# Routing in a fused two-block kernel: which engine computes the low parts of 32 weight pieces, and when the routing's steps and its turned indices come

## The chip, the cores and the metric

The kernel runs as one launch on one core of a Trainium2 chip. The metric is the device time in microseconds (us), the median of several executions; smaller is better. The core's engines each run their own instruction stream in order and wait for one another through semaphores: TensorE (PE, matmuls), VectorE (DVE), ScalarE (ACT), GpSimd (POOL) and SyncE (SP), which issues the loads.

## The reference, cut to what matters

Two transformer blocks on 256 tokens with model width 1024. The first ends in a mixture of 16,384 single-vector experts, and that part is the one touched:

```
q = (xt @ wq).reshape(T, 8, 2, 128)
s = einsum('thpd,hpnd->thpn', q, subkeys)             # 8 heads x 2 halves x 128 keys
top_s, top_i = top_k(s, 16)                           # lists of 16, sorted
cand_s = top_s[:,:,0,:,None] + top_s[:,:,1,None,:]    # 16 x 16 candidates a head
best_s, best_j = top_k(cand_s, 16)
idx = take_along_axis(cand_i, best_j); gates = softmax(best_s)
out = sum over the chosen: gelu(x . u_tab[idx]) * gates * v_tab[idx]
```

The kernel gathers nothing. It computes `gelu(x @ u_tab.T)` for all 16,384 experts, multiplies by a dense matrix of gates that is zero where an expert was not chosen, and multiplies by `v_tab`.

## The kernel before, in words

**Pieces.** Every weight streams through the core in pieces of 1 MB (128 partitions x 2048 numbers). To multiply in fp32, each piece is split in two: ScalarE copies it, rounded, into WH (the high part, L1341, helper `hi`), and another engine subtracts, `piece - WH`, into WL (the low part, helper `lo`, L1933 on VectorE, L2775 on GpSimd). Each part comes in two halves of 1024 numbers, one instruction for each half. TensorE then does 48 matmuls for a piece (L594), half of them after each half of the low part. WH and WL have two buffers, so the high part of piece p+2 can be written only when TensorE has used piece p. Three buffers take the loads of this stage. The function `low_on_gpsimd(name, j)` says which pieces have their low part on GpSimd.

**The stage.** `u` has 64 pieces of 256 experts. Pieces 0 to 31 (`up(0)`, `up(1)`) are multiplied while VectorE does the routing; pieces 48 to 63 (`up(3)`) while it builds the gates; then come `v` and the rest. In each program (tensor, scalar, vector) `up` is a generator with four steps to a piece. Where one of its steps takes a piece (`feed.take`), the split of the next piece is issued, so VectorE's low part of piece p+1 stands in its queue ahead of the routing that goes with piece p. ScalarE does a Gelu at a piece's end (L1670) and then the high part of the piece after next.

**Routing.** `routing()` of the vector program has 13 steps for each half of the tokens, 26 in all:
- steps 1 to 4: the sorted lists of the keys, four at a time: MAX8 (L2445), FIND_INDEX8 (L2448), MATCH_REPLACE8 (L2452) over 128 numbers
- steps 5 and 6: the candidates (a sum of 128x1024, L2464) and their sorted lists over 256 numbers; step 5 starts with a cast of the indices (L1921)
- step 7: the best scores less the first (L1906); ScalarE takes the exponent (L1333, its own routing step 7, which stands in its queue behind the Gelu of the seventh piece, and for the second half behind that of the twentieth); VectorE waits for it and divides
- steps 8 to 10 and 11 to 13: look up the two indices with wide one-hot tables of 128x2048: compare (L1906), multiply (L2492), sum (L2495)

One step goes with each piece. After piece 27 TensorE turns the indices and gates so that tokens lie along the free axis (`ids`, L1171), VectorE copies them (`ids`) and builds the first rows of the gates (`early_rows`, 20 steps, L2361 and L2367) beside pieces 28 to 31, at 1.25 steps for each step of `up`.

**Names below.** "Piece p" is the u piece of that number, from 0. "T6" is the time at which the Gelu of piece 6 starts, which is the end of that piece's matmuls.

Of the kernel before, what the change touches and what calls it, by code (L numbers as in the profile page):

```python
# [64 lines left out]
DOTS = ((0, 0, 0, 2, 0, 0, 0, 2, 0, 2, 0, 2), (0, 2, 0, 0) * 2 + (0, 2) * 2, (0, 2, 0, 0) * 2 + (0, 2) + (0,) * 6)  # L65
UNITS = ((2,) * 12, (1,) * 8 + (2,) * 4, (1, 0) * 5 + (1, 2, 2, 2, 2, 0))
HEADS = (3,) * 11 + (0,) * 5


def of_chunks(name, js):  # L70
# [117 lines left out]
class Marks:  # L188
# [5 lines left out]
    def on(self, name):  # L194
        if self.dry:
            return self.at.get(name, (self.zero, 1))
        return self.at[name]
# [62 lines left out]
class Mem:  # L260
# [42 lines left out]
    def tile(self, name):  # L303

        return self.ps[self.marks.bank.get(name, 0)][:, :]
# [156 lines left out]

def low_on_gpsimd(name, j):

    return name == "in_g" or name == "u" and j < 28 and j % 4 != 3


def split_views(m, n, name, j):
# [76 lines left out]
def chain(*gens):  # L545
    for g in gens:
        yield from g


def some(steps, n=1):  # L550
    for _ in range(n):
        next(steps, None)


def finish(steps):
    for _ in steps:
        pass


def beside(main, side, ratio):  # L560
    due = 0.0
    for _ in main:
        due += ratio
        while due >= 1:
            due -= 1
            next(side, None)


def tensor_program(q, m):
# [17 lines left out]
    def bank(name, of=ring):  # L587
        b = of["ids"][of["at"] % len(of["ids"])]
        of["at"] = (of["at"] + 1) % len(of["ids"])
        return give(b, name)  # L590

    def mm(o, pairs, start=True, stop=True, skip=False):
        for i, (l, r) in enumerate(pairs):
            ins = q.matmul(o, l, r, start=start and i == 0, stop=stop and i == len(pairs) - 1, skip_group_check=skip)  # L594
        return ins
# [60 lines left out]
    def proj(name, k0, *need, by=None):  # L656
        finish(proj_steps(name, k0, *need, by=by))
# [138 lines left out]
    def barrier(n):  # L796
        p.mark(("all", n, "pe"))
# [188 lines left out]
    def front():  # L986
# [54 lines left out]
        for i, _ in enumerate(states()):  # L1041
            some(fill, UNITS[2][i])
            some(dots, DOTS[2][i])
            some(at, HEADS[i])
            if i == 9:
# [46 lines left out]
    def up(b_):  # L1092

        for r in range(16):
            n, h, l, halves = take()
            tile = ("up", b_, r)
            b = bank(tile)
            for i, (x, z) in enumerate(halves):
                p.wait_ge(*on(("lo", n, i)))
                for e in range(2):  # L1100
                    fs = slice(e * P, (e + 1) * P)
                    ins = mm3(b[:, e * T:(e + 1) * T], [(h[:, k, fs], l[:, k, fs], RH[:, k, :], RL[:, k, :])
                                                        for k in range(x, z)], start=i == 0 and e == 0,
                              stop=i == 1 and e == 1, skip=True)
                    if e == 0:
                        yield
                ins.then_inc(*p.up(tile))
                p.mark(("used", n, i))
                yield

    def gate():

        for t in range(0, T, 4):
            b = bank(("gate", t), gate_ring).rearrange("p (i t) -> p i t", t=4)
            p.wait_ge(*on(("rows j", t // 8 * 8)))
            p.wait_ge(*on(("rows i", t)))
            for j in range(4):
                if t % 16 + j < 2:
                    l, r = m.early_j[:, t // 16, j, :], m.early_i[:, t // 16, j, :]
                else:  # L1120
                    l, r = m.rows_j[t // 8 % 2][:, t % 8 + j, :], m.rows_i[t // 4 % 3][:, j, :]
                ins = mm(b[:, :, j], [(l, r)])
            ins.then_inc(*p.up(("gate", t)))
            yield
# [24 lines left out]
    def peer():  # L1149
        proj("wq", 0, by="xs2")  # L1150
        feed.take()
        p.wait_ge(*m.loaded(CHUNKS.index(("sub", 0))))
        p.wait_ge(*on(("out", ("wq", 14))))
        sub = m.chunk(CHUNKS.index(("sub", 0)))
        for tt in range(2):
            for g in range(0, 16, 4):
                tile = ("keys", tt, g)
                b = bank(tile)
                for k in range(4):
                    ins = mm(b[:, k * P:(k + 1) * P], [(m.Qp[:, g + k, tt * P:(tt + 1) * P], sub[:, (g + k) * P:(g + k + 1) * P])])  # L1160
                ins.then_inc(*p.up(tile))
        p.mark("sub used")
        ring["ids"], ring["at"] = [0, 1, 2, 3], 0
        finish(up(0))
        steps = up(1)
        some(steps, 48)
        for tt in range(2):
            b = bank(("ids", tt))
            p.wait_ge(*on("routed"))
            for i in range(3):  # L1170
                ins = q.transpose(b[:, i * P:(i + 1) * P], m.res[tt][i], ident)  # L1171
            ins.then_inc(*p.up(("ids", tt)))
        finish(steps)
        g = gate()
        beside(up(3), g, 1)
        finish(g)
        for i in range(4):
            p.wait_ge(*on(("out", holder[4 + i])))
        finish(down(1))
        finish(up(2))  # L1180
        finish(down(0))
        finish(down(2))
        finish(down(3))
        for i in range(4):
            holder[4 + i] = ("down", i)
        banks = [bank(("turn back", k)) for k in range(0, 8, 2)]
        for tt in range(2):
            p.wait_ge(*on(("out", ("down", 2 * tt))))
            p.wait_ge(*on(("out", ("down", 2 * tt + 1))))
            for k in range(8):  # L1190
                o = k % 2 * T + tt * P
                ins = q.transpose(banks[k // 2][:, o:o + P], m.ot[:, tt, k * P:(k + 1) * P], ident)
                if tt == 1 and k % 2 == 1:
                    ins.then_inc(*p.up(("turn back", k - 1)))
        ring["ids"], ring["at"] = list(range(7)), 0
        barrier(2)
# [126 lines left out]
def scalar_program(q, m):  # L1323
# [110 lines left out]
    def front():  # L1434
# [107 lines left out]
        for i in range(16):  # L1542
            some(fill, UNITS[2][i])
            some(at, HEADS[i])
            some(dots, DOTS[2][i])
# [353 lines left out]
def vector_program(q, m):  # L1899
# [19 lines left out]
    def CP(o, x, name=None):  # L1919
        v.wait_ge(*v.last())  # L1920
        q.tensor_copy(o, x).then_inc(*v.up(name))  # L1921
# [16 lines left out]
    def proj(name, each=None):  # L1938
        finish(walk(name, feed, each))
# [29 lines left out]
    def rest_of_pair(tag, src, k):  # L1969

        v.wait_ge(*on((tag, "hi", k)))
        q.tensor_tensor(RL[:, k:k + 2, :], src[:, k:k + 2, :], RH[:, k:k + 2, :].bitcast(F32),
                        ALU.subtract).then_inc(*v.up((tag, "half", k // 4)))
        v.mark((tag, "pair", k // 2))
# [44 lines left out]
    def front():  # L2019
# [106 lines left out]
        for i, _ in enumerate(states()):  # L2126
            some(fill, UNITS[2][i])
            some(at, HEADS[i])
            some(dots, DOTS[2][i])
# [220 lines left out]
    def up(b_):  # L2350

        for _ in range(16):
            yield
            feed.take()
            yield
            yield
            yield
# [140 lines left out]
    def peer():  # L2498
        proj("wq")
        feed.take()  # L2500
        v.wait_ge(*on(("out", ("keys", 1, 12))))
        r = routing()
        beside(up(0), r, 0.25)
        steps = up(1)
        beside((next(steps) for _ in range(48)), r, 0.25)
        finish(r)
        for tt in range(2):
            t = ("ids", tt)
            ts = slice(tt * P, (tt + 1) * P)
            v.wait_ge(*on(t))  # L2510
            CP(m.ids[:, :, ts], tile(t)[:, 0:384].rearrange("p (a t) -> p a t", a=3), ("out", t))
        v.wait_ge(*v.last())
        early = early_rows()
        beside(steps, early, 1.25)
        finish(early)
        g = gate()
        beside(up(3), g, 1)
        finish(g)
        finish(down(1))
        finish(up(2))  # L2520
        g = far_gated()
        beside(down(0), g, 0.5)
        finish(g)
        finish(down(2))
        finish(down(3))
        for tt in range(2):
            v.wait_ge(*on(("down tokens", tt)))
            CP(m.ot[:, tt, 0:512], m.ps[4 + tt * 2][:, :], ("out", ("down", tt * 2)))
        for k in range(0, 10, 2):
            t = ("turn back", k)  # L2530
            if k < 8:
                v.wait_ge(*on(t))
                for g in range(2):
                    q.scalar_tensor_tensor(m.X[:, k + g, :], tile(t)[:, g * T:(g + 1) * T], mod[:, 40 + k + g:41 + k + g],
                                           m.X[:, k + g, :], ALU.mult, ALU.add).then_inc(*v.up(("x peer", k + g)))
                v.mark(("out", t))
            if k > 0:
                rest_of_pair("xs3", m.X, k - 2)
        v.mark("xs3")
        barrier(2)  # L2540
# [519 lines left out]
```

## Time and profile before

| | us |
|---|---|
| median of 3 executions | 1754.6 (1752.82 to 1759.29) |
| profiled execution, its own time | 1753.6 |
| its span | 1751.8 |
| TensorE busy | 1658.0 (95%) |
| VectorE busy | 1141.3 (65%) |
| ScalarE busy | 818.3 (47%) |
| GpSimd busy | 152.1 (9%), 58 low-part halves |

TensorE is busy nearly all the time, and the chain that ended last lies on it for 79% of the span. Its mean granted clock is 0.965 of full speed. What is left is the time in which it waits, or runs at the lower clock after a wait. GpSimd does nothing but low parts: 16 halves in an earlier stage and 42 in this one. Times in the rows count from the start of the span; the routing runs from 460 to 622 us, pieces 0 to 31 from 460 to 663.

### The profile page before, as it was taken

To read this page: it belongs to the slowest core of one execution; us is meant where nothing else is said; L and a number is where in the kernel's file an instruction comes from. 1 tells how busy PE (TensorE), PEld (TensorE's weight loads), DVE (VectorE), ACT (ScalarE), POOL (GpSimd) and SP (SyncE) were. 2 spreads that over 40 slices of the span, in tenths; PEclk is the share of its full clock that TensorE was granted. 3 is DMA by queue.
4 is the path that set the end of the run, shared out by engine and by line. 5 is a ranking of instruction groups with operands and counts; after the bars stand their busy time and mean duration, and the time that the engine had idled before them with its cause. 6 is when DMAs were issued, how large, how long until landed. Compare 5 with 4: busy or idle time off the path is not lost.

```text
span 1751.8 us, 27228 instructions
## 1 busy us (share of the span) xinstructions
PE 1658.0 (95%) x11462; PEld 1508.3 (86%) x11462; DVE 1141.3 (65%) x1961; ACT 818.3 (47%) x1187; POOL 152.1 (9%) x62
## 2 busy tenths in 40 slices
PE   6989999898989999999999999999999998999998
PEld 4879887798989999998889988888898787999996
DVE  5775865565497969997544477555575464556675
ACT  4635433334444444444444444444434655555663
POOL 0001231000356630000000000000000000000000
PEclk8999987899989999999999999999999998999999
DMA  9524323244435455455565586555655354445331
GB/s 388 209 103 150 140 97 121 97 145 144 169 123 190 169 171 175 166 175 181 192 224 185 181 288 234 195 193 196 256 190 175 116 180 145 165 137 183 121 123 70
DMA packets 48462, 300.57 MB, mean 172 GB/s; under 512 B 5586, under 2 KB 6098, under 8 KB 15827
## 3 DMA queue, kind: packets, MB, share of 16 engines
q1 hardware_dynamic: 43442, 290.28, 47.3%
q10 hardware_dynamic: 4896, 8.54, 1.3%
q8 instruction: 90, 1.47, 0.3%
q14 instruction: 34, 0.27, 0.0%
HBM read 288.18 MB, written 9.44 MB: 170 GB/s over the span
## 4 chain that ended last, share of the span: by engine, by line
PE 79%; DVE 13%; ACT 4%; POOL 2%; DMA 1%; issue 1%; SPq 0%; DVEq 0%; ACTq 0%
PE ps L594 78%; DVE WL L1933 3%; POOL WL L2775 2%; DVE ar L1906 2%; ACT ar L1333 1%; DVE ar L2448 1%; DVE ar L2445 1%; DVE ar L1917 1%; ACT WH L1341 1%; DVE ar L2452 1%; DVE ar L2232 1%; DMA vec<-in_vec 0%; DVE ar L1925 0%; DMA ar<-in_in_rkv 0%; DVE ar L2464 0%
## 5 line engine op out<-in xcount | busy, mean ns | idle before, releaser
L1933 DVE TENSOR_TENSOR WL<-ar,WH 128x1024 fp32r<-128x1024 f32 (+1 forms) x420 | 495.5, 1208 | 365.8 <-ACT WH L1341 365.2
L594 PE MATMUL ps<-RH,WH 128*128 128x256 f32 x2136 | 632.8, 296 | 34.7 <-DVE WL L1933 15.3
L594 PE MATMUL ps<-RL,WH 128*128 128x256 f32 x2136 | 614.5, 288 | 0.0
L594 PE MATMUL ps<-RH,WL 128*128 128x256 f32 x2136 | 614.1, 287 | 0.0
L1341 ACT ACTIVATE WH<-ar 128x1024 fp32r<-128x1024 f32 (+1 forms) x478 | 481.8, 1041 | 274.7 <-PE ps L594 258.6
L594 PEld LDWEIGHTS ps<-RH,WH 128*128 128x128 f32 x2136 | 420.0, 197 | 42.5 <-issue 12.7
L594 PEld LDWEIGHTS ps<-RL,WH 128*128 128x128 f32 x2136 | 420.1, 197 | 0.9 <-issue 0.2
L594 PEld LDWEIGHTS ps<-RH,WL 128*128 128x128 f32 x2136 | 419.6, 196 | 0.0
L594 PE MATMUL ps<-WH,RH 128*128 128x512 f32 (+1 forms) x832 | 325.5, 391 | 11.3 <-DVE ar L1917 5.9
L594 PE MATMUL ps<-WL,RH 128*128 128x512 f32 (+1 forms) x832 | 322.0, 387 | 0.0
L594 PE MATMUL ps<-WH,RL 128*128 128x512 f32 (+1 forms) x832 | 321.7, 387 | 0.0
L594 PE MATMUL ps<-ar 128*128 128x128 f32 (+8 forms) x2124 | 246.4, 299 | 21.5 <-DVE ar L1921 10.9
L594 PEld LDWEIGHTS ps<-ar 128*128 128x128 f32 (+6 forms) x2124 | 204.8, 177 | 48.7 <-issue 27.2
L594 PEld LDWEIGHTS ps<-WH,RH 128*128 128x128 f32 x832 | 157.5, 189 | 45.0 <-DVE ar L1917 6.0
L2775 POOL TENSOR_TENSOR WL<-ar,WH 128x1024 fp32r<-128x1024 f32 x58 | 151.9, 2642 | 476.0 <-ACT WH L1341 476.0
L594 PEld LDWEIGHTS ps<-WL,RH 128*128 128x128 f32 x832 | 157.7, 190 | 31.6 <-issue 1.0
L594 PEld LDWEIGHTS ps<-WH,RL 128*128 128x128 f32 x832 | 157.6, 189 | 31.7
L1670 ACT ACTIVATE ar<-ps 128x512 f32<-128x512 f32 x64 | 38.2, 597 | 178.2 <-PE ps L594 178.2
L1333 ACT ACTIVATE ar<-ps 128x256 f32<-128x256 f32 (+3 forms) x156 | 71.9, 461 | 92.3 <-PE ps L594 78.3
L1906 DVE TENSOR_TENSOR ar<-ps,ar 128x512 f32<-128x512 f32 (+3 forms) x59 | 38.4, 651 | 65.1 <-PE ps L594 58.4
L2361 DVE TENSOR_SCALAR ar<-con,ar 128x128 f32<-128x128 f32 x256 | 71.3, 340 | 0.0
L1333 ACT ACTIVATE ar<-ar,small 128x128 f32<-128x128 f32 (+1 forms) x48 | 21.9, 455 | 62.2 <-DVE small L1994 61.4
(155 smaller groups left out, 956.1 us busy)
## 6 DMA issues: line engine op xcount, KB each, us to landing
ar<-in_u SPq DMA_DIRECT2D x64, 1024.0 KB, 4.9
ar<-in_v SPq DMA_DIRECT2D x64, 1024.0 KB, 4.9
ar<-in_adr SPq DMA_DIRECT2D x16, 1024.0 KB, 5.3
ar<-in_ada SPq DMA_DIRECT2D x8, 1024.0 KB, 12.7
ar<-in_in_g SPq DMA_DIRECT2D x8, 1024.0 KB, 4.9
ar<-in_wq SPq DMA_DIRECT2D x8, 1024.0 KB, 4.9
far_gates<-ar ACTq DMA_DIRECT2D x32, 256.0 KB, 2.3
ar<-far_gates SPq DMA_DIRECT2D x16, 512.0 KB, 3.9
```

What stands on the lines that cost most here:

```text
L594: ins = q.matmul(o, l, r, start=start and i == 0, stop=stop and i == len(pairs) - 1, skip_group_check=skip)
L1333: q.activation(o, x, f, **k).then_inc(*a.up(name))
L1341: q.activation(h[:, x:z, :], src[:, x:z, :], ACT.Copy).then_inc(*a.up(("hi", n, i)))
L1670: q.activation(m.H[:, i0:i0 + 2, :], tile(t).rearrange("p (n t) -> p n t", n=2), ACT.Gelu).then_inc(*a.up(("out", t)))
L1906: q.tensor_tensor(o, x, y, op).then_inc(*v.up(name))
L1917: q.scalar_tensor_tensor(o, x, s, y, op0, op1).then_inc(*v.up(name))
L1933: q.tensor_tensor(l[:, x:z, :], src[:, x:z, :], h[:, x:z, :].bitcast(F32), ALU.subtract).then_inc(*v.up(("lo", n, i)))
L2232: q.scalar_tensor_tensor(x, x, 1.0, m.cwide, ALU.mult, ALU.mult, accum_out=mod[:, i:i + 1]).then_inc(*v.up(("adr", j)))
L2361: return q.tensor_scalar(o, cst("iota"), m.ids[:, 0, t:t + 1], m.ids[:, 2, t:t + 1], ALU.is_equal, ALU.mult)
L2445: q.max(vals[:, s8], src).then_inc(*v.up())
L2448: q.max_index(idx[:, s8], vals[:, s8], src).then_inc(*v.up())
L2775: q.tensor_tensor(l[:, x:z, :], src[:, x:z, :], h[:, x:z, :].bitcast(F32), ALU.subtract).then_inc(*g.up(("lo", n, i)))
```

## The change

Four edits, all in how work is placed:
- GpSimd's pieces: before all but every fourth of pieces 0 to 27 (21 pieces); now pieces 0 to 7 and 12 to 20 (17 pieces). VectorE has pieces 8 to 11 and 21 to 31 (before 3, 7, 11, 15, 19, 23, 27 to 31).
- The routing steps on VectorE go by a table: one with each of pieces 0 to 9, three with piece 10, one with each of 11 to 18, none with piece 19, one with each of 20 to 24.
- TensorE turns the indices after piece 25, and VectorE waits for them there.
- The early rows go beside pieces 26 to 31 at 0.875 a step.

ScalarE's program has the same order as before. The file's lines move down by 3 to 5.

```diff
+ROUTED = (1,) * 10 + (3,) + (1,) * 8 + (0,) + (1,) * 5
 def low_on_gpsimd(name, j):
-    return name == "in_g" or name == "u" and j < 28 and j % 4 != 3
+    return name == "in_g" or name == "u" and (j < 8 or 12 <= j < 21)
@@ tensor program
         steps = up(1)
-        some(steps, 48)
+        some(steps, 40)
@@ vector program
         r = routing()
-        beside(up(0), r, 0.25)
-        steps = up(1)
-        beside((next(steps) for _ in range(48)), r, 0.25)
+        steps = chain(up(0), up(1))
+        for n in ROUTED:
+            some(steps, 4)
+            some(r, n)
         finish(r)
+        some(steps, 4)
...
         early = early_rows()
-        beside(steps, early, 1.25)
+        beside(steps, early, 0.875)
```

VectorE's queue where the first half of the tokens passes from the sorted lists to the look-ups, before. L1933 is a low part (piece 7's in the fourth row), L2473 is the first instruction behind ScalarE's exponent:

```order
L2452 MATCH_REPLACE ar<-ar 128x256 x4
L2445 MAX ar<-ar 128x8 x4
L2448 MAX_INDEX ar<-ar 128x8 x4
L1933 TENSOR_TENSOR WL<-ar,WH 128x1024 x2
L1906 TENSOR_TENSOR ar<-ar 128x128
L2473 TENSOR_REDUCE small<-ar 128x8
L1925 RECIPROCAL small<-small 128x8
L1906 TENSOR_TENSOR ar<-ar,small 128x128
L2483 TENSOR_SCALAR ar<-ar 128x128
L1921 CAST ar<-ar 128x128
L1906 TENSOR_TENSOR ar<-ar,con 128x2048
L2492 TENSOR_TENSOR ar<-ar 128x2048
```

The same place now (L1936 is the low part, of pieces 8 and 9 here; the other lines are 3 higher too):

```order
L2455 MATCH_REPLACE ar<-ar 128x256 x4
L2448 MAX ar<-ar 128x8 x4
L2451 MAX_INDEX ar<-ar 128x8 x4
L1909 TENSOR_TENSOR ar<-ar 128x128
L2476 TENSOR_REDUCE small<-ar 128x8
L1928 RECIPROCAL small<-small 128x8
L1909 TENSOR_TENSOR ar<-ar,small 128x128
L1936 TENSOR_TENSOR WL<-ar,WH 128x1024 x2
L2486 TENSOR_SCALAR ar<-ar 128x128
L1924 CAST ar<-ar 128x128
L1909 TENSOR_TENSOR ar<-ar,con 128x2048
L1936 TENSOR_TENSOR WL<-ar,WH 128x1024 x2
```

No low part stands among the lists now; the first one (piece 8's) stands behind the four instructions around the exponent, and each look-up step has one ahead of it.

VectorE's queue at the same place for the second half of the tokens, before (the low part is that of piece 23):

```order
L1906 TENSOR_TENSOR ar<-ar 128x128
L2473 TENSOR_REDUCE small<-ar 128x8
L1925 RECIPROCAL small<-small 128x8
L1906 TENSOR_TENSOR ar<-ar,small 128x128
L2483 TENSOR_SCALAR ar<-ar 128x128
L1921 CAST ar<-ar 128x128
L1906 TENSOR_TENSOR ar<-ar,con 128x2048
L2492 TENSOR_TENSOR ar<-ar 128x2048
L1933 TENSOR_TENSOR WL<-ar,WH 128x1024 x2
L2495 TENSOR_REDUCE ar<-ar 128x128
```

And now (the low parts are those of pieces 21, 22 and 23):

```order
L1909 TENSOR_TENSOR ar<-ar 128x128
L2476 TENSOR_REDUCE small<-ar 128x8
L1928 RECIPROCAL small<-small 128x8
L1909 TENSOR_TENSOR ar<-ar,small 128x128
L2486 TENSOR_SCALAR ar<-ar 128x128
L1924 CAST ar<-ar 128x128
L1909 TENSOR_TENSOR ar<-ar,con 128x2048
L1936 TENSOR_TENSOR WL<-ar,WH 128x1024 x2
L2495 TENSOR_TENSOR ar<-ar 128x2048
L1936 TENSOR_TENSOR WL<-ar,WH 128x1024 x2
L2498 TENSOR_REDUCE ar<-ar 128x128
L1936 TENSOR_TENSOR WL<-ar,WH 128x1024 x2
```

Piece 21's low part has come from GpSimd into VectorE's queue, behind the exponent and the first wide comparison. On TensorE six transposes stand 96 matmuls (two pieces) sooner, and nothing else moved there.

## Rows read from the trace of the kernel before

**Rows 1.** Busy time of each engine by stretch, then granted clock, DMA share, GB/s.
```profile
500.00:520.00 20.00, 12.23 (x85) 12.22 (x85) 19.35 (x41) 7.86 (x9) 7.12 (x3) 0.74 0.31 106
580.00:600.00 20.00, 17.82 (x135) 17.53 (x134) 19.31 (x43) 10.35 (x12) 13.61 (x5) 0.91 0.46 154
620.00:640.00 20.00, 18.66 (x157) 18.67 (x157) 6.69 (x7) 8.57 (x11) 8.29 (x4) 1.00 0.60 206
680.00:700.00 20.00, 20.00 (x175) 20.00 (x174) 20.00 (x49) 8.77 (x15) 0.00 (x0) 1.00 0.53 174
```
**Rows 2.** TensorE's waits, 459 to 664 us: total, times, longest.
```profile
PE ps L594 <- DVE WL L1933: 7.8, 1, 7.8
PE ps L594 <- POOL WL L2775: 4.6, 4, 2.2
```
**Rows 3.** Timeline of ScalarE: start, length, instruction, [idle before, releaser].
```profile
465.53 0.60 ACT L1670 ACTIVATE ar<-ps 128x512 f32<-128x512 f32 x1 [3.86 <-PE ps L594]
...
500.08 0.60 ACT L1670 ACTIVATE ar<-ps 128x512 f32<-128x512 f32 x1 [3.27 <-PE ps L594]
500.76 1.28 ACT L1333 ACT_TABLE_LOAD   x1
509.16 0.31 ACT L1333 ACTIVATE ar<-ar 128x128 f32<-128x128 f32 x1 [7.12 <-DVE ar L1906]
509.38 1.99 ACT L1341 ACTIVATE WH<-ar 128x1024 fp32r<-128x1024 f32 x2
...
515.98 0.60 ACT L1670 ACTIVATE ar<-ps 128x512 f32<-128x512 f32 x1 [3.31 <-PE ps L594]
...
586.17 0.60 ACT L1670 ACTIVATE ar<-ps 128x512 f32<-128x512 f32 x1 [3.46 <-PE ps L594]
...
601.57 0.60 ACT L1670 ACTIVATE ar<-ps 128x512 f32<-128x512 f32 x1 [5.32 <-PE ps L594]
...
638.90 0.60 ACT L1670 ACTIVATE ar<-ps 128x512 f32<-128x512 f32 x1 [3.27 <-PE ps L594]
...
645.30 0.60 ACT L1670 ACTIVATE ar<-ps 128x512 f32<-128x512 f32 x1 [3.91 <-PE ps L594]
...
662.58 0.60 ACT L1670 ACTIVATE ar<-ps 128x512 f32<-128x512 f32 x1 [3.27 <-PE ps L594]
```
**Rows 4.** Timeline of VectorE, 472 to 520 us.
```profile
472.86 2.36 DVE L1933 TENSOR_TENSOR WL<-ar,WH 128x1024 fp32r<-128x1024 f32 x2 [2.87 <-ACT WH L1341]
475.26 0.87 DVE L2445 MAX8 ar<-ar 128x8 f32<-128x128 f32 x4
...
480.07 0.88 DVE L2445 MAX8 ar<-ar 128x8 f32<-128x128 f32 x4
...
484.89 2.09 DVE L1921 CAST ar<-ar 128x256 f32<-128x256 uint32 x1
487.02 3.31 DVE L2464 TENSOR_TENSOR ar<-ar 128x1024 f32<-128x1024 f32 x1
...
497.85 1.23 DVE L2464 TENSOR_TENSOR ar<-ar 128x1024 f32<-128x1024 f32 x1
...
506.46 2.34 DVE L1933 TENSOR_TENSOR WL<-ar,WH 128x1024 fp32r<-128x1024 f32 x2
...
512.99 4.38 DVE L1906 TENSOR_TENSOR ar<-ar,con 128x2048 f32<-128x2048 f32 x1
517.41 2.29 DVE L2492 TENSOR_TENSOR ar<-ar 128x2048 f32<-128x2048 f32 x1
519.73 2.29 DVE L2495 TENSOR_REDUCE ar<-ar 128x128 f32<-128x2048 f32 x1
```
**Rows 5.** Timeline of GpSimd: low parts of pieces 4 and 5, and of 9 and 10.
```profile
478.67 4.79 POOL L2775 TENSOR_TENSOR WL<-ar,WH 128x1024 fp32r<-128x1024 f32 x2 [6.75 <-ACT WH L1341]
484.43 4.82 POOL L2775 TENSOR_TENSOR WL<-ar,WH 128x1024 fp32r<-128x1024 f32 x2 [0.97 <-ACT WH L1341]
...
517.61 11.45 POOL L2775 TENSOR_TENSOR WL<-ar,WH 128x1024 fp32r<-128x1024 f32 x4 [2.38 <-ACT WH L1341]
```

## The prediction

> **What bounds the kernel now.** I read the stretches first: TensorE should show where it is not full. In three of them it is not [rows 1]: 12.23 of 20 us with the clock at 0.74, then 17.82 at 0.91, then 18.66 at 1.00. From 680 us on it is full again, and VectorE too. Its waits come next: all of them between 459 and 664 us are for low parts, 7.8 us once for VectorE and 4.6 us in four waits for GpSimd [rows 2]. So in this stage neither loads nor high parts come last, only low parts.
>
> Then the Gelus, which mark the ends of pieces [rows 3]. T0 is 465.53 and T6 is 500.08, so a piece without a wait takes 34.55/6 = 5.76 us. Pieces 1 to 31 would take 31 x 5.76 = 178.6 us; they took 662.58 - 465.53 = 197.05. So 18.5 us are lost here, and that is all that this change can give in the stage. They split so: piece 7 took 15.90, lost 10.1; pieces 20 and 21 took 15.40, lost 3.9; piece 28, behind which the turning of the indices stands, took 6.40, lost 0.6; the rest, 3.9, is spread over pieces 9, 12, 19, 22, 24 and 25.
>
> The timelines of VectorE and GpSimd say why [rows 4, 5]. Piece 7's low part is VectorE's. TensorE wanted it at 500.08, and it started at 506.46, since in VectorE's queue it stands behind the candidates and their lists, which ran late. The wait costs 7.8; the other 2.3 are the lower clock after it (0.74 over 20 us is 5.2 us lost at full-speed count, of which about half fell into the wait itself). And ops of VectorE with two inputs in the core's memory take turns with GpSimd's: the sum of 128x1024 took 1.23 alone and 3.31 beside a low part of GpSimd, the comparison of 128x2048 took 4.38 where the multiplication took 2.29, and the latter held GpSimd up in its turn (four halves in 11.45 instead of 2 x 4.79 = 9.58). The sorted lists don't take turns: four MAX8 took 0.87 with GpSimd idle and 0.88 beside the low part that ran from 478.67 to 483.46. Nor does the sum of the look-up, 2.29 with GpSimd busy.
>
> The Trainium skill (SBUF — State Buffer, section "Who interferes with whom") says that an instruction of VectorE with two inputs there contends with GpSimd's reads. By that rule FIND_INDEX8 and MATCH_REPLACE8, if their loaded values count as a second input, would contend too, and this change, which puts GpSimd beside all the lists, would slow them. The list step from 480.07 to 484.89 had GpSimd beside it most of the time and took 4.82; the one from 475.26 to 480.07 had it for 1.4 us and took 4.81. The trace decides: no contention.
>
> **The change part by part.** I carry the schedule on with durations of these rows. VectorE: low part 2.34 to 2.36 for both halves (1.2 each), list step over 128 numbers 4.82, over 256 numbers 497.85 - 490.33 = 7.5, look-up 2.29, with two small ones of about 0.25 ahead of each comparison. GpSimd: 2.4 a half, 4.8 a piece, starting 1.6 us after T (484.43 against T3 = 482.8). VectorE can give the first half of a low part at T+2.8.
>
> *Pieces 3 and 7 to GpSimd.* 4.8 us a piece against 5.76: GpSimd keeps up, its first half at T+4.0, 1.8 before it is wanted. VectorE loses the low part of piece 3 and the wait ahead of it (2.36 + 2.87 [rows 4]), so step 5 starts at 484.89 - 5.2 = 479.7. Its cast waits for GpSimd until 481.06 (as in the row), its sum until 483.46 and ends about 484.5; lists to 492.0. Step 6: the sum waits 0.6 for the half that began at 490.2, ends 493.7; lists to 501.2. GpSimd, held up 1.1 by this sum, ends piece 7's first half at 498.4 and its second at 500.8: before 500.08 and 503.0, when TensorE wants them. So T7 = 500.08 + 5.76 = 505.84, and the 10.1 us go.
>
> *The exponent.* ScalarE has its table loaded at 502.04 at the earliest [rows 3], VectorE's scores are there at 501.5. Exponent 502.04 to 502.35, high part of piece 8 to 504.3, low part on VectorE 503.4 to 505.8, first half at 504.6. Wanted at 505.84: no wait. ScalarE's wait of 7.12 goes too.
>
> *Pieces 8 to 11 on VectorE between the look-ups.* Each piece now needs on VectorE a low part and a look-up, 2.35 + 2.29 = 4.6, with a comparison 5.2, under 5.76, and nothing of GpSimd's beside it. Following it: piece 9's low part ends 511.0 (T8 = 511.6), 10's 515.7, 11's 521.4 (T10 = 523.1). The three steps with piece 10 end at 528.9. The comparison and the multiplication there hold GpSimd from 524.8 to 526.5, so piece 12's first half comes at 528.9, just when TensorE wants it (T11 = 528.9). I take 0.1 us lost. The losses at pieces 9 and 12 go.
>
> *Lists of the second half.* No low part on VectorE until piece 21, so it runs ahead: from 528.9, 4 x 4.82, then two candidate steps with turns of 2 to 4 us, in all to about 569. Then it waits for the exponent, which stands on ScalarE behind the Gelu of piece 19: T19 = 528.95 + 8 x 5.76 = 575.0, Gelu 0.6, table 1.28, exponent from 577.0 to 577.3. **Here is the new wait.** Piece 21's low part is queued behind it: the rest of step 20 to 578.2, the small ones and the comparison to 581.1, low part's first half at 582.3. TensorE wants it at T20 = 580.8 and starts about 582.4: 1.6 us lost. A wait of 2.2 at most was followed by a slower clock before (0.91 over 580 to 600, or 3.6 us at half speed, 1.8 lost), one inside 620 to 640 was not, with 1.34 us idle at clock 1.00 [rows 1, 2]. 1.6 lies between: 0 to 1.8, I take 0.9. What went away here: the 3.9 of pieces 20 and 21, and the late ones of 22, 24 and 25, all due to GpSimd taking turns with look-ups; pieces 22 to 26 now go by the 4.6 to 5.2 of VectorE and catch up, the last look-up ending at about 606, T25 at about 611.
>
> *Turning two pieces sooner.* The indices are ready 5 us ahead of T25, so TensorE doesn't wait. The 0.6 of piece 28 comes with piece 26. VectorE copies, then has six low parts (14.1) and 20 early steps (13.4, from 0.26 us a row and 1.2 a comparison) in six pieces, 34.6: fits. It can start the gates' rows a little before T31 instead of just after; in the gates' stage TensorE and VectorE are both full [rows 1], so I count 0, at most 0.6.
>
> *Loads* wait for the low part three pieces back. That of a GpSimd piece ends at T+6.4 where VectorE's ended at T+3.9; a load takes about 5 us (page, DMA issues), and the high part wants it 17 us after that T: hidden, with 5 us in hand.
>
> **Sum.** Lost before 18.5; lost after 0.6 + 0.1 + 1.6 + 0.9 = 3.2. Gain 15.3. The profiled execution had 1753.6, so 1738.3; the median of the runs is 1.0 above that execution and their lowest 0.8 below it. I say 1738.5. All later stages are ordered by the same engines and move as a block. The case's own range, with the clock from 0 to 1.8, the gates' 0.6, and 1.5 for a median of other executions: 1735.5 to 1741.
>
> **Rivals.**
> 1. *The exponent of the first half is late.* Four ops ahead of it take turns (cast, two sums, scores); I counted 3.8 us of turns, the most is 4 x 2.4 = 9.6. Then the scores come at 507, piece 8's high part waits behind the exponent, and its low part's first half comes at 508.7 against 505.84: 2.9 lost, and about 1.9 by the clock. Gain 10.5: 1743. For it: in the row both ops at 484.89 and 487.02 waited a full turn. Against: the second sum at 497.85 met none, and GpSimd is idle when the scores come.
> 2. *The look-ups with low parts between them bind.* VectorE, not TensorE, sets the pace of pieces 8 to 11 and 21 to 31, since each low part must wait for its high part and each look-up for the one before. The price is what a piece on VectorE takes over 5.76; it decides at 16/15 = 1.1 us a piece over, i.e. 6.8. At 7.3 (as piece 25 had) 15 x 1.55 = 23 lost against 15.3 won: slower, 1761. For it: 19.35 of 20 us busy on VectorE [rows 1]. Against: the row's own durations give 5.2, and much of that busy time is turns.
> 3. *It only moves the wait.* The second exponent costs the whole of what pieces 20 and 21 lost and more, since the rest of step 20 and the comparison stand ahead of the low part: a wait of 4 with 2.5 of clock, and the same at piece 12. Gain 15.3 + 2.5 - 2 x 5 = 8: 1746. Against: nothing in the rows makes the comparison longer than 2.3 without GpSimd.
>
> The Trainium skill (GPSIMD Engine Reference, section "Key points") says that VectorE is structurally about twice as fast at elementwise work. The trace agrees, 1.2 against 2.4 us a half; it matters only where GpSimd has no slack, and by the rows it has 1.0 a piece.
>
> **Chances.** Forecast 0.76; rival 1 0.12; rival 3 0.08, half of it under the bound of 0.5% (8.8 us, about what a measurement of this kernel can tell from no change); rival 2 0.02; 0.02 for anything else, as a later stage giving the time back. Faster 0.93, same 0.05, slower 0.02. Range, to take in most of rival 1: 1735 to 1743.5.
>
> **What would show it.** Piece 7 at 5.8 us; ScalarE's exponent within 2.5 us of the seventh Gelu; MAX8 and the rest of the lists at the same length beside GpSimd; wide comparisons and multiplications at 2.29 and not 4.38; a single wait of TensorE for VectorE, 1 to 2 us, at piece 21; T31 near 647.4. It is wrong if piece 8 or 12 shows a wait over 1 us, if pieces 22 to 25 take over 6, or if the gates' stage takes longer than 9.31 us a piece.

## The result, and the profile after

| | before | after |
|---|---|---|
| first comparison, median of 7 each (us) | 1757.33 (1752.37 to 1759.29) | 1744.41 (1738.02 to 1748.25) |
| ratio, 95% interval | | 0.9929 (0.9914 to 0.9945) |
| second comparison, ratio | | 0.9934 (0.9909 to 0.9959) |
| profiled execution, its own time | 1753.6 | 1747.57 |

The kernel got faster by 0.7%. The forecast was 1738.5 with a range to 1743.5, so the measured 1744.41 lies 0.9 above the range and 5.9 above the forecast. Inside the stage nearly every number of the forecast came out.

TensorE's waits from 470 to 660 us in the changed kernel (columns as in [rows 2]):

```profile
PE ps L597 <- ACT WH L1344: 1.6, 1, 1.6
```

Five waits of 12.4 us in all [rows 2] have become one of 1.6. ScalarE around the first exponent, piece 12, and the second exponent (to set beside [rows 3]):

```profile
509.57 0.60 ACT L1673 ACTIVATE ar<-ps 128x512 f32<-128x512 f32 x1 [3.27 <-PE ps L597]
510.25 1.28 ACT L1336 ACT_TABLE_LOAD   x1
511.55 0.31 ACT L1336 ACTIVATE ar<-ar 128x128 f32<-128x128 f32 x1
511.76 1.99 ACT L1344 ACTIVATE WH<-ar 128x1024 fp32r<-128x1024 f32 x2
513.77 1.28 ACT L1673 ACT_TABLE_LOAD   x1
515.34 0.60 ACT L1673 ACTIVATE ar<-ps 128x512 f32<-128x512 f32 x1 [0.28 <-PE ps L597]
...
538.37 0.60 ACT L1673 ACTIVATE ar<-ps 128x512 f32<-128x512 f32 x1 [3.26 <-PE ps L597]
...
544.41 0.60 ACT L1673 ACTIVATE ar<-ps 128x512 f32<-128x512 f32 x1 [3.55 <-PE ps L597]
...
584.74 0.60 ACT L1673 ACTIVATE ar<-ps 128x512 f32<-128x512 f32 x1 [3.27 <-PE ps L597]
585.41 1.28 ACT L1336 ACT_TABLE_LOAD   x1
586.70 0.31 ACT L1336 ACTIVATE ar<-ar 128x128 f32<-128x128 f32 x1
586.92 1.99 ACT L1344 ACTIVATE WH<-ar 128x1024 fp32r<-128x1024 f32 x2
588.93 1.28 ACT L1673 ACT_TABLE_LOAD   x1
590.49 0.60 ACT L1673 ACTIVATE ar<-ps 128x512 f32<-128x512 f32 x1 [0.28 <-PE ps L597]
590.99 2.00 ACT L1344 ACTIVATE WH<-ar 128x1024 fp32r<-128x1024 f32 x2
598.05 0.60 ACT L1673 ACTIVATE ar<-ps 128x512 f32<-128x512 f32 x1 [5.06 <-PE ps L597]
```

T6 is 509.57 here and T7 515.34: piece 7 takes 5.77 where it took 15.90. The exponent follows the Gelu and the table at once, with no wait for VectorE (7.12 before). Piece 12 takes 6.04 and piece 21 takes 598.05 - 590.49 = 7.56. VectorE at the same places ([rows 4]):

```profile
489.14 1.57 DVE L1924 CAST ar<-ar 128x256 f32<-128x256 uint32 x1
490.74 3.31 DVE L2467 TENSOR_TENSOR ar<-ar 128x1024 f32<-128x1024 f32 x1
494.09 1.41 DVE L2448 MAX8 ar<-ar 128x8 f32<-128x256 f32 x4
...
501.57 1.61 DVE L2467 TENSOR_TENSOR ar<-ar 128x1024 f32<-128x1024 f32 x1
...
510.69 0.29 DVE L1909 TENSOR_TENSOR ar<-ar 128x128 f32<-128x128 f32 x1
511.89 0.28 DVE L2476 TENSOR_REDUCE small<-ar 128x8 f32<-128x128 f32 x1 [0.91 <-ACT ar L1336]
...
517.97 2.35 DVE L1936 TENSOR_TENSOR WL<-ar,WH 128x1024 fp32r<-128x1024 f32 x2
520.36 2.29 DVE L2495 TENSOR_TENSOR ar<-ar 128x2048 f32<-128x2048 f32 x1
...
587.05 0.29 DVE L2476 TENSOR_REDUCE small<-ar 128x8 f32<-128x128 f32 x1 [6.67 <-ACT ar L1336]
...
588.46 2.29 DVE L1909 TENSOR_TENSOR ar<-ar,con 128x2048 f32<-128x2048 f32 x1
590.67 2.35 DVE L1936 TENSOR_TENSOR WL<-ar,WH 128x1024 fp32r<-128x1024 f32 x2
```

The look-ups take 2.29 between low parts. The cast and the first sum wait for GpSimd, the second sum for 0.4. The scores are ready 1.4 us after T6. For the second half of the tokens VectorE waits 6.67 for the exponent, and the comparison and then the low part of piece 21 stand behind it. TensorE wanted that low part at 590.5 and its first half ended at 591.9. The list of waits names ScalarE's high part, but that of piece 21 had been done since 588.9; what came last is the low part, as the run with the two exchanged shows below. GpSimd beside the first lists, and the two pieces after the look-ups ([rows 5]):

```profile
488.16 4.81 POOL L2780 TENSOR_TENSOR WL<-ar,WH 128x1024 fp32r<-128x1024 f32 x2 [0.98 <-ACT WH L1344]
493.92 4.77 POOL L2780 TENSOR_TENSOR WL<-ar,WH 128x1024 fp32r<-128x1024 f32 x2 [0.95 <-ACT WH L1344]
...
534.24 11.09 POOL L2780 TENSOR_TENSOR WL<-ar,WH 128x1024 fp32r<-128x1024 f32 x4 [24.02 <-ACT WH L1344]
```

It has 0.95 to 0.99 us in hand at a piece beside the lists. It is held up at three places: half a piece took 3.41 instead of 2.41 beside the second sum of each half of the tokens, and beside the look-ups that go with piece 10 four halves took 11.09 instead of 9.6. Behind piece 21's wait the clock stayed up (columns of [rows 1]):

```profile
590.00:592.00 2.00, 0.45 (x4) 0.25 (x4) 2.00 (x3) 1.72 (x4) 0.00 (x0) 1.00 0.00 0
592.00:594.00 2.00, 1.97 (x16) 2.00 (x17) 1.97 (x2) 0.98 (x2) 0.00 (x0) 1.00 0.00 0
594.00:596.00 2.00, 2.00 (x19) 2.00 (x18) 2.00 (x2) 0.00 (x0) 0.00 (x0) 1.00 0.95 291
```

The Gelus are counted on through the gates' stage: its 16 pieces end at T32 to T47, and behind T47 the multiplication by `v` begins (the down stage, below). Four parts make up a profiled execution: T0; the stage, T31 - T0; the gates' stage, T47 - T31, which is 148.6 before and 148.0 after in every profile (the gates start 0.59 sooner); and what lies behind T47.

| | T0 | T31 - T0 | behind T47 | T0 and behind T47 together |
|---|---|---|---|---|
| before, first profile | 465.53 | 197.05 | 940.62 | 1406.15 |
| after, first profile | 475.01 | 181.27 | 941.39 | 1416.40 |

The stage and the gates gave 15.78 + 0.59 = 16.4 us; the rest of the kernel, with the same instructions, took 10.2 us more. Ten of the sixteen runs below go to that question.

### The profile page after: what moved, and what is told of

It reads as the page before. It is cut to its first block, busy times and chain, and to the rows that moved or that the text cites. A ratio compares the mean times of both kernels' runs of the same rounds, so it can differ in the third digit from the quotient of the medians.

```text
span 1745.7 us, 27230 instructions
## 1 busy us (share of the span) xinstructions
PE 1670.6 (96%) x11462; PEld 1514.7 (87%) x11462; DVE 1138.4 (65%) x1969; ACT 819.4 (47%) x1187; POOL 123.8 (7%) x54
## 4 chain that ended last, share of the span: by engine, by line
PE 86%; DVE 8%; ACT 4%; DMA 2%; issue 1%; SPq 0%; DVEq 0%; ACTq 0%
PE ps L597 85%; DVE WL L1936 2%; DVE ar L1909 2%; ACT ar L1336 1%; DVE ar L1920 1%; DMA ar<-in_cwide 1%; ACT WH L1344 1%; DMA vec<-in_vec 0%; PE ps L778 0%; DMA ar<-in_in_rkv 0%; DVE ar L2235 0%; DVE ar L1928 0%; DVE ar L2065 0%; DVE RL L1952 0%; ACT L1336 0%
## 5 line engine op out<-in xcount | busy, mean ns | idle before, releaser
L1936 DVE TENSOR_TENSOR WL<-ar,WH 128x1024 fp32r<-128x1024 f32 (+1 forms) x428 | 503.4, 1205 | 347.7 <-ACT WH L1344 346.9
L597 PE MATMUL ps<-ar 128*128 128x128 f32 (+8 forms) x2124 | 255.9, 312 | 19.2 <-DVE ar L1924 10.1
L597 PEld LDWEIGHTS ps<-ar 128*128 128x128 f32 (+6 forms) x2124 | 210.1, 183 | 50.9 <-issue 31.4
L2780 POOL TENSOR_TENSOR WL<-ar,WH 128x1024 fp32r<-128x1024 f32 x50 | 123.6, 2494 | 461.4 <-ACT WH L1344 461.4
```

Of the source, the lines that this page charges most:

```text
L1936: q.tensor_tensor(l[:, x:z, :], src[:, x:z, :], h[:, x:z, :].bitcast(F32), ALU.subtract).then_inc(*v.up(("lo", n, i)))
L2780: q.tensor_tensor(l[:, x:z, :], src[:, x:z, :], h[:, x:z, :].bitcast(F32), ALU.subtract).then_inc(*g.up(("lo", n, i)))
```

## The experiments

The stage's length repeats to 0.04 us over seven profiles of the changed kernel and to 0.8 us over five of before (196.3 or 197.1, by what piece 7 takes), so the stage's theories are told apart by one profile; the medians of whole executions are far coarser.

| kernel | T31 - T0 | pieces over 5.8 us | ratio to before, interval |
|---|---|---|---|
| before, 5 profiles | 196.26 to 197.06 | 7, 9, 12, 19 to 22, 24, 25, 28 | 0.9996 (0.998 to 1.0011) |
| after, 7 profiles | 181.25 to 181.29 | 12, 21, 26 | 0.9934 (0.9909 to 0.9959) |
| e3, pieces only | 179.47 | 12, 28 | 0.9898 (0.9873 to 0.9923) |
| e4, steps only | 194.83 | 7, 9, 12, 19 to 22, 24, 26 | 0.9994 (0.998 to 1.0007) |
| e5, piece 7 only | 194.31 | 7, 8, 9, 12, 19 to 22, 24, 25, 28 | 0.9996 (0.998 to 1.0011) |
| e6, comparison behind low part | 179.46 | 12, 26 | 0.9907 (0.9884 to 0.993) |
| e7, also piece 12 | 179.20 | 26 | 0.9911 (0.9893 to 0.993) |
| e8, GpSimd beside look-ups | 211.87 | 14 pieces | 1.0081 (1.0055 to 1.0106) |

The lengths of pieces go by the Gelus. Where ScalarE is late itself, a part of a wait is counted one piece too early: before the change piece 20 shows 7.59, though TensorE's wait of 2.18 us stands ahead of piece 21.

**The pieces alone (e3).** The kernel before with

```diff
-    return name == "in_g" or name == "u" and j < 28 and j % 4 != 3
+    return name == "in_g" or name == "u" and (j < 8 or 12 <= j < 21)
```

> Only the pieces' engines change (GpSimd has 0 to 7 and 12 to 20); one routing step with each piece and the turning behind piece 27 stay as before. Theory (all of the gain is in which pieces GpSimd has, and the changed kernel's one wait, at piece 21, comes from a table that puts the wide comparison ahead of piece 21's low part): here the low part stands ahead of the comparison, so no wait at piece 21. T31 - T0 = 178.6 + 0.3 (piece 12) + 0.6 (turning) = 179.5; gates' start 0.6 later than in the changed kernel; in all 1 us faster than the changed kernel. Rival (the step table and the earlier turning carry a part of the gain): T31 - T0 of 184 or more.

Measured 179.47, and no wait at piece 21: the theory. One of the four edits carries all of the stage's gain, and more: the changed kernel's step table costs it 1.8 us. What the earlier turning gives is the 0.59 at the gates' start, which e3 lacks.

**The steps and the turning alone (e4).** The changed kernel with the pieces' rule of before and `ROUTED = (1,) * 20 + (2,) + (1,) * 4`.

> The pieces' engines stay as before; only the steps and the turning move: one routing step with each of pieces 0 to 19, two with 20, one with 21 to 24, turning behind piece 25, early rows at 0.875. (The changed kernel's own table would wait in a ring here: it puts step 20, which waits for ScalarE behind the Gelu of piece 19, ahead of piece 19's low part on VectorE.) Theory (the pieces carry the gain): piece 7 takes 15.9 as before, T31 - T0 = 197 within 3, the gates' start 0.6 sooner; the time is that of before within 3 us. Rival (turning sooner carries a part): T31 - T0 under 193.

Piece 7 took 15.22, the stage 194.83, the gates came 0.6 sooner, and the ratio is that of no change: the theory. Against the 196.3 of before with the same piece 7, 1.4 us go, mainly at piece 25, whose low part no longer comes late.

**Piece 7 alone (e5).** The kernel before with `j < 28 and (j % 4 != 3 or j == 7)`.

> The kernel before with only piece 7 given to GpSimd beside its others. Theory (the wait of 7.8 at piece 7 goes only in part, since VectorE, with piece 3's low part still among the lists and turns with GpSimd, has the scores at 506.5 on the scale of before, and piece 8's high part waits on ScalarE behind the exponent): piece 7 takes 5.8, piece 8 about 12 (wait 4.8, clock 2), so T31 - T0 is 3 to 4 us shorter than 197.05. Rival (the low part of piece 7 was all of it): piece 8 takes 5.8 and T31 - T0 is 10 us shorter.

TensorE's waits, and ScalarE around the exponent:

```profile
PE ps L594 <- POOL WL L2775: 9.6, 4, 5.3
```

```profile
501.36 0.60 ACT L1670 ACTIVATE ar<-ps 128x512 f32<-128x512 f32 x1 [3.27 <-PE ps L594]
502.04 1.28 ACT L1333 ACT_TABLE_LOAD   x1
508.55 0.31 ACT L1333 ACTIVATE ar<-ar 128x128 f32<-128x128 f32 x1 [5.23 <-DVE ar L1906]
508.76 1.99 ACT L1341 ACTIVATE WH<-ar 128x1024 fp32r<-128x1024 f32 x2
```

The wait moved as the theory has it: from piece 7's low part (7.8) to piece 8's (5.3), whose high part stands on ScalarE behind an exponent that waits for VectorE. The rival falls, but the gain is smaller than forecast: 2 to 2.7 us instead of 3 to 4, since the wait was 5.3 and not 4.8. The single marks misled: by the Gelus piece 7 took 10.70 and piece 8 took 8.52, where 5.8 and 12 were expected. Piece 7's Gelu came late since ScalarE was held, though TensorE had ended piece 7 in time and waited from 507.1 to 512.4. So moving piece 7 isn't enough. That moving piece 3 as well would be is the prediction's working (2.36 + 2.87 us on VectorE against an exponent that is 5.2 late here); no run moved these two alone.

**The comparison behind the low part (e6).** The changed kernel with

```diff
-ROUTED = (1,) * 10 + (3,) + (1,) * 8 + (0,) + (1,) * 5
+ROUTED = (1,) * 10 + (3,) + (1,) * 7 + (0, 0, 1, 2) + (1,) * 3
```

> The changed kernel with another step table: no step with pieces 18 and 19, one with 20, two with 21, one with 22 to 24, so that piece 21's low part stands ahead of the first wide comparison and the turning stays behind piece 25. Theory (the wait of 1.6 us at piece 21 is the comparison's 2.8 us ahead of the low part, not the exponent itself): piece 21 takes 5.76, T31 - T0 = 179.5, the gates' start as in the changed kernel; 1.8 us faster than it. Rival (the exponent itself, behind the twentieth Gelu, holds the high part of piece 21): piece 21 still takes 7 or more.

VectorE behind the second exponent:

```profile
584.61 0.29 DVE L2476 TENSOR_REDUCE small<-ar 128x8 f32<-128x128 f32 x1 [6.68 <-ACT ar L1336]
...
585.56 2.36 DVE L1936 TENSOR_TENSOR WL<-ar,WH 128x1024 fp32r<-128x1024 f32 x2
...
588.48 2.29 DVE L1909 TENSOR_TENSOR ar<-ar,con 128x2048 f32<-128x2048 f32 x1
```

Against the twentieth Gelu the exponent and the high part stand where they stood, the low part comes 2.7 us sooner, and piece 21 takes 5.76. The wait was the order of two things on VectorE.

**Piece 12 as well (e7).** From e6, with `13 <= j < 21` and `ROUTED = (1,) * 10 + (2, 2) + (1,) * 6 + (0, 0, 1, 2) + (1,) * 3`.

> The table of the run before that puts piece 21's low part ahead of the comparison, and piece 12's low part on VectorE between two of the look-up steps of pieces 10 and 11 (two steps with each). Theory (the 0.28 at piece 12 are the two wide look-ups that hold GpSimd up): no piece but the turning one over 5.8, T31 - T0 = 178.6 + 0.6 = 179.2, gain over before 197.05 - 179.2 + 0.6 = 18.4 us, or a ratio of 0.9895. Rival (VectorE has no room for a fifth low part among the look-ups): piece 12 or 13 takes over 6.5.

Only piece 26, with the turning ahead of it, is over 5.8; the stage takes 179.20, as forecast, and would take 178.6 without any wait. In ratio it can't be told from e3 and e6. These three all have a lower median than the changed kernel (1739.84, 1738.8 and 1741.04 against 1744.61), with intervals that overlap its own. The differences, 3.6 to 5.8, are larger than the 1.8 to 2.1 of the stage; with these intervals that stays open.

**GpSimd beside the look-ups (e8).** The changed kernel with `8 <= j < 12 or 21 <= j < 28` and e4's table.

> The mirror image: GpSimd has pieces 8 to 11 and 21 to 27, beside the look-ups, and VectorE 0 to 7 and 12 to 20, beside the sorted lists (steps and turning as in the run with the steps only). Theory (lists and low parts add up on VectorE, 4.8 + 2.4 against 5.76 a piece, and look-ups take turns with GpSimd's halves at 4.4 instead of 2.3): lows and lists alone take VectorE 51 us to the end of step 6, so piece 7 waits 11 us or more, the second half as much; T31 - T0 over 210, slower than before by 13 or more. Rival (where GpSimd's pieces lie doesn't matter, only that piece 7 and 3 are not VectorE's): within 5 us of before.

TensorE's waits, and VectorE's first comparison:

```profile
PE ps L597 <- DVE WL L1936: 19.2, 7, 5.3
PE ps L597 <- POOL WL L2780: 4.1, 6, 1.2
```

```profile
515.62 2.40 DVE L1924 CAST ar<-ar 128x128 f32<-128x128 uint32 x1
518.05 4.39 DVE L1909 TENSOR_TENSOR ar<-ar,con 128x2048 f32<-128x2048 f32 x1
```

The stage takes 15 us longer than before and the whole 13 us, as forecast. Both halves of the reason show: the lists with low parts on VectorE run late (19.2 us of waits), and beside GpSimd the comparison takes 4.39 again. The place was not quite as forecast: instead of one wait of 11 us at piece 7 there were 1.1, 5.3 and 2.8 us ahead of pieces 5, 6 and 7.

**The same two kernels again.** First a second comparison of the two, with one more profile of each.

> The kernel before, unchanged. The question is what one execution's time owes to stages that the change doesn't touch: the changed kernel's profiled execution had its first piece's Gelu (T0) 9.5 us later than the profiled execution of before (475.01 against 465.53), with the same instructions ahead of it. Theory (the time ahead of T0 differs from execution to execution by how long TensorE's clock stays low after waits, whatever the kernel): T0 of this profile lies anywhere from 464 to 476, T31 - T0 is 197.05 within 0.5, and the ratio to before is 1.000 within 0.003. Rival (the placement of the change itself makes the time ahead of T0 longer): T0 here is within 2 us of 465.5.

> The changed kernel, unchanged. Theory (the time ahead of T0 is drawn anew each time): T0 anywhere from 464 to 476, T31 - T0 = 181.3 within 0.5, and a ratio between 0.990 and 0.994, a gain of 15.8 in the stage and 0.6 at the gates' start, or 16.4 of 1757. Rival (the change makes the stretch ahead of T0 slower): T0 again near 475, and a gain of 12 or less.

T0 came at 469.27 and 467.74: the 475.01 of the first profile after was not the change's doing, but differs from execution to execution. The ratio, 0.9934, lies in the theory's range; the gain of 11.6 that it stands for is also the rival's "12 or less", and that is taken up below. Then single executions with a profile, first three of the changed kernel and one of the kernel before, with these expectations:

> One more execution of the changed kernel, for the spread between executions. Theory (all stages around the routing differ between executions by the clock after waits alone, whatever the kernel, and piece 21's wait of 1.6 us is short enough to leave the clock up): T31 - T0 = 181.3 and piece 21 7.56; T0 between 465 and 476. Rival (piece 21's wait brings the clock down in some executions, which would explain a measured gain 3 to 4 us under the 16.4 that stage and gates show): piece 21 takes 9.0 to 9.5 in one or more of the four.

> As the run before: theory T31 - T0 = 181.3 each time, T0 between 465 and 476; rival piece 21 at 9.0 to 9.5 in some.

> As the two runs before: theory T31 - T0 = 181.3 each time, T0 between 465 and 476; rival piece 21 at 9.0 to 9.5 in some.

> The kernel before once more. Theory: T0 between 465 and 476 as for every kernel, T31 - T0 between 196.2 and 197.1 by the clock after piece 7's wait. Rival (the changed kernel's placement makes the stretch ahead of T0 longer): T0 within 2 us of 465.5 to 469.3.

All seven profiles of the changed kernel in the end have piece 21 at 7.55 to 7.57, so the rival of the first three falls. The profile of before had T0 at 472.05 and a stage of 196.27, so its rival falls too. Two more of each kernel were for a further question:

> The kernel before again. Open: outside of the stage (all but T0 to T47) five executions of the changed kernel had 1407.9 to 1416.4 us, mean 1412.6, three of before 1406.1 to 1411.1, mean 1409.0; is it chance or the change? Theory (chance, by the clock after waits ahead of T0 and behind T47, whatever the kernel): with two or three more of each the means come within 2 us. Rival (the change shifts the phase of what follows so that the clock falls more often at the start of the down stage and at 983 us): the difference stays at 3 or more, and the part behind T47 is 941 with the changed kernel and 940 or less before.

> As the run before, the changed kernel: theory a time outside of the stage of 1410.9 within 5, from the same spread as before; rival 1412 or more, with 941 or more behind T47.

> The kernel before again, the same question: theory 1410.9 within 5 outside of the stage; rival 1410 or less, with 940 or less behind T47.

> The changed kernel again, the same question: theory 1410.9 within 5 outside of the stage; rival 1412 or more, with 941 or more behind T47.

| | T0 | behind T47 |
|---|---|---|
| before, 5 | 465.5, 469.3, 472.1, 472.9, 467.1: mean 469.4 | mean 939.4 (937.0 to 940.6) |
| after, 7 | 475.0, 467.7, 469.6, 472.2, 472.8, 469.5, 464.2: mean 470.1 | mean 941.1 (940.2 to 942.0) |
| the six others | 466.3 to 473.9, mean 470.5 | mean 939.9 (938.1 to 941.1) |

Ahead of T0 no difference is seen (0.7 us in the mean, where single profiles lie 7 to 11 apart). Behind T47 the changed kernel has 1.7 us more in the mean. Together the means differ by 2.5, between the theory's 2 and the rival's 3; the part behind T47 came as the rival has it, 941.1 against 939.4. With so few profiles it isn't settled. Much of it is seen in the granted clock. One stretch ahead of T0, of the first profiles before and after and of the second after:

```profile
260.00:280.00 20.00, 17.37 (x159) 13.27 (x157) 13.06 (x39) 7.78 (x24) 0.00 (x0) 0.83 0.14 48
```

```profile
260.00:280.00 20.00, 18.76 (x111) 12.76 (x110) 11.23 (x32) 6.37 (x21) 0.70 (x1) 0.50 0.02 9
```

```profile
260.00:280.00 20.00, 19.47 (x124) 14.02 (x124) 11.34 (x32) 5.89 (x18) 0.00 (x0) 0.50 0.00 1
```

0.50 is the lower of the clock's two levels. The second after has the low clock here too and still reached T0 7.3 us sooner than the first, so one stretch doesn't decide. Nor does the granted clock show all: within the first 30 us it stands at 1.00 in the changed kernel's first profile, and yet sixteen matmuls took 1.93 us there that took 1.07 before:

```profile
23.23 1.07 PE L594 MATMUL ps<-ar 128*32 128x256 f32 x16
```

```profile
24.60 1.93 PE L597 MATMUL ps<-ar 128*32 128x256 f32 x16
```

Now the wait of 2.4 us with which the down stage begins. It ended at 814.5 before and at 807.6 after; the stretches behind it:

```profile
814.00:817.00 3.00, 2.54 (x11) 2.14 (x12) 2.75 (x4) 2.00 (x3) 0.00 (x0) 1.00 0.04 14
```

```profile
808.00:811.00 3.00, 3.00 (x9) 2.27 (x9) 2.65 (x3) 1.12 (x2) 0.00 (x0) 0.54 0.00 0
```

After the same wait the clock stays up once and falls to half once, which costs 1.5 us. It fell in 2 of 5 profiles of before, in 6 of 7 of the changed kernel, in e4 and e5, and in none of e3, e6, e7 and e8. A second such place lies 180 us later, at the rival's 983 us, behind a wait of 1.9 us. Here the clock fell in the first profile of before and stayed up in the second:

```profile
998.00:1001.00 3.00, 3.00 (x9) 2.31 (x9) 2.22 (x4) 0.83 (x1) 0.00 (x0) 0.53 0.01 3
```

```profile
1003.00:1006.00 3.00, 3.00 (x15) 2.45 (x15) 2.92 (x4) 1.07 (x1) 0.00 (x0) 1.00 0.06 12
```

It costs 1.6 us and fell in 2 of 5 profiles of before and 5 of 7 of the changed kernel. By these counts the two places make up 0.7 + 0.5 = 1.2 of the 1.7 us behind T47. Whether the change makes the falls likelier or this is chance stays open.

## Why the prediction was wrong

**Right, step by step.** Piece 7: forecast 5.76, measured 5.77. Scores 1.4 us after T6: 1.4. Exponent at once. Pieces 8 to 11 without a wait: so. Piece 12: forecast 0.1 lost, measured 0.28. Piece 21: wait forecast 1.6, measured 1.58; for the clock 0.9 was taken, and it stayed at 1.00 (beyond its wait the piece took 0.2 more). Pieces 22 to 25 at 5.76. The turning 0.6: 0.64. In sum 3.2 lost, measured 2.7; T31 - T0 forecast 181.8, measured 181.27. The gates' start was counted 0, at most 0.6: it is 0.59. Rivals 1, 2 and 3 fell: the lists and turns of GpSimd were as read, and the pieces kept 5.76 us with look-ups between VectorE's low parts. The sums and comparisons took 1.6 to 4.4 beside GpSimd against 1.2 and 2.3 alone, as the Trainium skill (SBUF — State Buffer, "Who interferes with whom") has it; the reading of that rule by which the lists would contend too fell, since GpSimd's low parts beside them kept 4.8 us and the scores came when forecast.

**The step that failed** is the last part of the sum: "The profiled execution had 1753.6, so 1738.3; the median of the runs is 1.0 above that execution", "All later stages are ordered by the same engines and move as a block", and "1.5 for a median of other executions". The gain was subtracted from one execution, as if what lies outside of the stage were fixed. It is not. Over 18 profiles of eight kernels it runs from 1404.4 to 1416.4, mean 1410.3, standard deviation 3.4, in part since the granted clock falls after some waits in one execution and not in the next. The profile of before had 1406.15, 2.6 under the mean of its kernel's five (1408.8), and the three times shown had a median 2.7 under that of seven (1754.6 against 1757.33).

The miss of 5.9 us adds up so. The median of before was 1757.33, 3.7 above the profiled execution, of which the forecast had taken 0.2: 3.5 too low. The stage and the gates took 1.1 less than forecast. The remaining 3.5 are time outside of the stage that the changed kernel's median has and the forecast put at nothing: its gain is 12.9 in the medians, and 16.4 in stage and gates. With the mean of all 18 profiles in the base's place the forecast's own stage gives 1410.3 + 181.8 + 148.6 + 1.8 (time outside the span) = 1742.5, inside the range but still 1.9 under the measured time. The margin of 1.5 was too narrow where single executions deviate by 3.4 and the base is one of them.

**What is left.** The stage's gain against all profiles of before is 196.7 - 181.3 + 0.6 = 16.0; the ratios give 12.5 (9.7 to 15.1) and 11.6 (7.2 to 16.0). The 1.7 us behind T47, if they are the change's, bring 16.0 to 14.3, which both intervals hold; the rest can't be told from the differences between executions. The other kernels don't show such a lack as clearly: stage and gates against the ratio are 17.2 and 17.9 for e3, 17.8 and 16.3 for e6, 18.1 and 15.6 for e7. So it stays open whether the changed kernel pays something outside of the stage or was unlucky in its falls of the clock.

## What to carry to other kernels

Where two engines take turns at the memory, give the slower one its work beside the operations that don't take part, and look at the order inside the faster one's queue: the piece rule alone gave all of the stage's gain, and one comparison ahead of a low part gave 1.8 us of it back. Follow a stage by the marks of its pieces, which repeat to 0.1 us where no long wait stands ahead of them, and forecast the stage from them; forecast the whole from the mean of several executions, and take the range from how the rest of the kernel varies, not from one profile. A mark on an engine that is itself held up is not the end of the work that it marks.

## What the runs showed of the hardware that was not expected

- The time outside of the stage comes in steps. Over all 18 profiles, between the same two instructions of ScalarE (times of the first profile of before), it was 22.9 to 23.0 or 24.6 us (203.5 to 226.5), then 10.4, 14.5 or 15.2 to 15.5 (269.4 to 279.8), 10.0 or 11.45 to 11.6 (811.2 to 821.2), and 12.95 or 14.6 (989.6 to 1004.2), with nothing between. The steps aren't independent: the eight profiles with 24.6 at the first place are the eight with 15.2 to 15.5 at the second.
- The length of a wait doesn't say by itself whether the clock falls, nor does a longer wait make it surer. A wait of 2.41 us before the down stage left it at 1.00 in 8 of 18 profiles and brought it to about half in 10, between the same instructions; one of 1.93 us, 180 us later, brought it down in 11 of 18. Waits of 2.18 us before piece 21 brought it down in all seven profiles that have them (before, e4, e5); 1.58 us before piece 21 left it up in seven of seven.
